# Inverting the 64x64 triangular blocks of a chunked recurrence on 32x32 corners, one PSUM bank a product, with even and odd steps side by side

## The reference

```
proj = h @ w_in                      # h: normed, scaled input
# recurrence, 8 heads of 64, one state of 64x64 a head (rwkv7):
for t in range(1024):
    sa = state @ a_t
    state = state * w_t + sa b_t^T + v_t k_t^T
    y_t = state @ r_t
# and beside it attention over a band of 9 chunks of 64 tokens, 8 heads
x = x + gate * (concat(y_r * silu(g_r), y_a * silu(g_a)) @ w_out)
```

## Time and profile before

| | |
|---|---|
| median of 3 runs | 2421.11 us (2420.31 to 2425.67) |
| profiled execution, own time | 2418.48 us |
| its span, first to last instruction | 2416.6 us |
| PE busy | 2277.8 us, 94% |
| DVE busy | 1456.7 us, 60% |
| ACT busy | 937.6 us, 39% |
| mean granted clock of PE | 0.972 of 2.4 GHz |

### The profile page before, as it was taken

One profiled execution on the slowest core, in us unless ns is written; L12 is line 12 of the kernel. 1 busy time (PEld: TensorE's weight loads), 2 busy tenths in 40 slices (PEclk: granted clock), 3 DMA queues, 4 the chain that ended last, 5 costly groups with the idle time before them and its releaser, 6 DMA issues. The chain is left out here.

```text
span 2416.6 us, 43216 instructions
## 1 busy us (share of the span) xinstructions
PE 2277.8 (94%) x18830; PEld 1848.8 (77%) x18830; DVE 1456.7 (60%) x2456; ACT 937.6 (39%) x1532; POOL 78.7 (3%) x61
## 2 busy tenths in 40 slices
PE   7999988999999999999999999999999998789789
PEld 5777767788888888888878888778777776567667
DVE  5575866565434886777753454646455655767743
ACT  4446432444333443333342433354333232335441
POOL 0000000000000000000000000002000001200000
PEclk9999989999999999999999999989999999799989
DMA  5332252544123232222365534333323113111044
GB/s 179 88 94 66 69 170 71 173 123 129 53 62 119 77 96 83 79 79 86 93 196 164 157 90 135 98 113 110 109 80 107 51 37 97 41 44 44 3 129 150
DMA packets 329349, 238.15 MB, mean 99 GB/s; under 512 B 10948, under 2 KB 288580, under 8 KB 329032
## 3 DMA queue, kind: packets, MB, share of 16 engines
q1 hardware_dynamic: 326424, 229.82, 31.7%
q10 hardware_dynamic: 2736, 5.57, 0.6%
HBM read 202.33 MB, written 33.03 MB: 97 GB/s over the span
## 5 line engine op out<-in xcount | busy, mean ns | idle before, releaser
L1525 PE MATMUL PS<-SR 128*128 128x512 f32 (+2 forms) x1696 | 681.6, 402 | 43.2 <-DVE SR L2106 34.8
L1526 PE MATMUL PS<-SR 128*128 128x512 f32 (+2 forms) x1696 | 659.9, 389 | 0.0
L1527 PE MATMUL PS<-SR 128*128 128x512 f32 (+2 forms) x1696 | 659.7, 389 | 0.0
L2106 DVE TENSOR_TENSOR SR<-SB,SR 128x1024 fp32r<-128x1024 f32 (+1 forms) x240 | 289.1, 1206 | 289.8 <-ACT SR L2967 289.5
L1525 PEld LDWEIGHTS PS<-SR 128*128 128x128 f32 (+1 forms) x1696 | 320.4, 189 | 128.3 <-DVE SR L2106 36.9
L1527 PEld LDWEIGHTS PS<-SR 128*128 128x128 f32 (+1 forms) x1696 | 320.2, 189 | 68.7
L1526 PEld LDWEIGHTS PS<-SR 128*128 128x128 f32 (+1 forms) x1696 | 320.9, 189 | 62.2 <-issue 1.7
L2967 ACT ACTIVATE SR<-SB 128x1024 fp32r<-128x1024 f32 (+1 forms) x240 | 247.5, 1033 | 254.9 <-DMA SB<-in_w_down 116.1
L1546 PE MATMUL PS<-SR 128*128 128x512 f32 x624 | 243.4, 390 | 0.3 <-DVE SR L2232 0.3
L1548 PE MATMUL PS<-SR 128*128 128x512 f32 x624 | 242.8, 389 | 0.0
L1547 PE MATMUL PS<-SR 128*128 128x512 f32 x624 | 242.7, 389 | 0.0
(11 more groups left out here) (315 smaller groups left out, 3032.2 us busy)
## 6 DMA issues: line engine op xcount, KB each, us to landing
SB<-in_w_in SPq DMA_DIRECT2D x110, 512.0 KB, 4.0
SB<-in_w_up SPq DMA_DIRECT2D x88, 256.0 KB, 3.3
SB<-in_w_out SPq DMA_DIRECT2D x32, 512.0 KB, 4.2
SB<-in_w_down SPq DMA_DIRECT2D x32, 512.0 KB, 4.1
SB<-in_w_ada SPq DMA_DIRECT2D x12, 1024.0 KB, 5.2
hidden<-SB SPq DMA_DIRECT2D x22, 512.0 KB, 3.4
SB<-hidden SPq DMA_DIRECT2D x43, 256.0 KB, 5.3
asides<-SB SPq DMA_DIRECT2D x36, 256.0 KB, 4.1
```

The lines of the kernel that those rows point to most:

```text
L1525: pe.matmul(out, whi[:, k - k0, :], hi[k], start=(k == 0), stop=False)
L1526: pe.matmul(out, whi[:, k - k0, :], lo[k], start=False, stop=False)
L1527: i = pe.matmul(out, wlo[:, k - k0, :], hi[k], start=False, stop=(k == j.K - 1))
L2106: v.tensor_tensor(m.f32r(a, kn * cn), m.f32(a, kn * cn), m.f32r(a + 1024, kn * cn).bitcast(F32), SUB).then_inc(*on("split.v", p))
```

## The change

- The inverse is built on 32x32 diagonal blocks in four levels (l = 0..3), with T and TT as compact tiles `Tc` and `TTc` (four 32-row diagonal corners, 256 columns each) in a tile `TB` of their own, and X in `Xc`. A last step (`pre_up` and `pre_add` with l = 4) makes the off-diagonal 32x32 corner of each 64x64 block from the two diagonal ones.
- Each product is 32 matmuls of 32x32 (the last `pre_add` 16) into one PSUM bank, and one DVE instruction of 256 columns drains it. `pre_i` and `pre_t0` go; `pre_mm` makes both M and its transpose on the corners, 64 matmuls in place of 16, and DVE masks them in two instructions and adds the identity in one.
- `pre_own` is new on ACT: four copies of 32 rows from `TTc` into the block diagonal of TT. `pre_add` at l = 4 has one small copy on DVE and one on ACT. `pre_zero` is new on POOL: it clears TT first.
- `seq_u` waits for the three writers of TT.
- `pres(0, 2, 4, 6)` and `pres(1, 3, 5, 7)` are two generators. KN is still one tile, so only one cp at a time is between `pre_kn` and `pre_v` (`masking`).
- The planner's costs of these steps are new, and the projections of k1 and v1 wait for `("read", 2)` and `("read", 3)`.

```diff
-        self.m2, M = f32(X0 + 6656, 640), f32(X0 + 7296, 512)
+        self.m2, TB = f32(X0 + 6656, 352), f32(X0 + 7296, 512)
+        self.TB = [TB, self.fixed["cst"][:, CST["mst"][0]:CST["mst"][0] + 512]]
+        self.Xc = [work(27904, 256), work(28416, 256)]
-        "pre_turn": [("pe", 0.67), ("v", 0.84)], ...
+        "pre_up": [("pe", 0.5), ("v", 0.45)], "pre_add": [("pe", 0.5), ("v", 0.45)], "pre_turn": [("pe", 0.5), ("v", 0.45)], ...
 # Order.pre
-        for l in range(5):
-            yield from one(("pre_up", cp, l), "pre.v", "X", cp, l)
-            if l < 4:
-                yield from one(("pre_turn", cp, l), "pre.v", "T", cp, l)
-            yield from one(("pre_add", cp, l), "pre.v", "TT", cp, l)
+        for l in range(4):
+            yield from single(("pre_up", cp, l), ("pre.v", "X", cp, l))
+            yield from single(("pre_turn", cp, l), ("pre.v", "T", cp, l))
+            yield from single(("pre_add", cp, l), ("pre.v", "TT", cp, l))
+        yield [("pre_own", cp)]
+        yield from single(("pre_up", cp, 4), ("pre.v", "X", cp, 4))
+        yield from single(("pre_add", cp, 4), ("pre.v", "TT", cp, 4), ("pre.a", "far", cp))
 # compose
-                  self.seqs(), self.pres(), ...
+                  self.seqs(), self.pres(0, 2, 4, 6), self.pres(1, 3, 5, 7), ...
 # PE: 32 corners a product
+    def corners():
+        return [(par, j, h, d, slice(64 * h + 32 * d, 64 * h + 32 * d + 32)) for j in range(4) for par in range(2) for h in range(2)
+                for d in range(2)]
+    def pre_turn(cp, l, b, free):
+        w.wait_ge(*at("pre.v", "X", cp, l))
+        w.wait_ge(*at("pre.v", "TT", cp, l - 1))
+        out = corner(b, free)
+        for par, j, h, d, ps in corners():
+            x = pe.matmul(out(ps, par, j), m.TTc[cp % 2][ps, par, j], Xc(cp, ps, par, j), start=True, stop=True)
 # DVE: one instruction in place of two
-        for f in range(2):
-            T = side(m.per[cp % 2]["KN"][:, 0:512], f)
-            v.tensor_tensor(T, side4(bank(got[f][0])), T, ADD).then_inc(*on("pre.v", "T", cp, l, f))
+        v.tensor_tensor(m.Tc[cp % 2], corner(b), m.Tc[cp % 2], ADD).then_inc(*on("pre.v", "T", cp, l))
```

More of the change, by code:

```diff
@@ L693, in flow @@
                 late = max(late, self.placed(step, end if chained else ready))
-                if step[0] not in ("pre_x", "pre_add", "pre_i"):
+                if step[0] not in ("pre_x", "pre_own") and (step[0] != "pre_add" or step[2] == 4):
                     end = late
@@ L1306, in one, with single @@
             yield [use2(step, *release)]
-        yield [("g_load", cp)]
+        def single(step, *releases):
+            yield from self.room((P8, 1))
+            b, free = P8.take()
+            P8.give(b, *releases)
+            yield [(*step, b, free)]
+        yield [("g_load", cp), ("pre_zero", cp)]
         for i in range(2):
@@ L1405, in lora_of @@
         if half:
-            yield from self.after("lo1", "clear", ("read", 3))
+            yield from self.after("lo1", "clear", ("read", 2), ("read", 3))
         else:
@@ L1977, in pre_v @@
             *on("pre.pe", "v", cp))
-    def pre_up(cp, l, got):
-        r = m.per[cp % 2]
-        w.wait_ge(*(at("pre.v", "T", cp, l - 1, 1) if l else at("pre.v", "T", cp)))
-        for par, a, jl, f in crossing(got):
-            j, c, ps = 2 * f + jl, par ^ f, half(par ^ a ^ f)
-            x = pe.matmul(bank(got[f][0])[half(par ^ a), 128 * par + 64 * jl:128 * par + 64 * jl + 64], both(r["AR"])(c, 0, j)[ps, :],
-                          head(r["KN"])(c, 0, j)[ps, :], start=True, stop=True)
-        x.then_inc(*on("pre.pe", "up", cp, l))
@@ L2940, in vector_program @@
               band_y=band_y, mun=mun, prep_a=prep_a, prep_b=prep_b, prep_bon=prep_bon, pre_ar=pre_ar,
-              pre_mm=pre_mm, pre_kn=pre_kn, pre_i=pre_i, pre_t0=pre_t0, pre_up=pre_up, pre_turn=pre_turn, pre_add=pre_add, seq_0=seq_0, seq_x=seq_x, seq_z=seq_z,
+              pre_mm=pre_mm, pre_kn=pre_kn, pre_up=pre_up, pre_turn=pre_turn, pre_add=pre_add, seq_0=seq_0, seq_x=seq_x, seq_z=seq_z,
               seq_mean=seq_mean, seq_var=seq_var, seq_norm=seq_norm, band_p=band_p, seq_out=seq_out, fin_part=fin_part)
@@ L3330, in pre_x, with pre_own, pre_add @@
             S.also("pre.a", "x", cp, 1)
+    def pre_own(cp):
+        w.wait_ge(*at("pre.v", "TT", cp, 3))
+        w.wait_ge(*at("pre.g", "zero", cp))
+        TT = m.per[cp % 2]["TT"].rearrange("p (a j t) -> p a j t", a=2, j=4)
+        for h in range(2):
+            for d in range(2):
+                ps = slice(64 * h + 32 * d, 64 * h + 32 * d + 32)
+                i = a.activation(TT[ps, :, :, 32 * d:32 * d + 32], m.TTc[cp % 2][ps], ACT.Copy)
+        i.then_inc(*on("pre.a", "own", cp))
+    def pre_add(cp, l, b, free):
+        if l == 4:
+            w.wait_ge(*at("pre.pe", "add", cp, 4))
+            w.wait_ge(*at("pre.g", "zero", cp))
+            a.activation(h8(m.per[cp % 2]["TT"])[0:32, :, 32:64], h8(bank(b)[:, 0:256])[0:32], ACT.Copy).then_inc(*on("pre.a", "far", cp))
     def pre_v(cp, got):
@@ L3407, in seq_gain, with pre_zero @@
         g.tensor_tensor(y, y, q, ADD).then_inc(*on("seq.g", "y", cp))
-    do = dict(mark=lambda name: S.mark("g", name), load=load, prep_a=prep_a, prep_b=prep_b, seq_gain=seq_gain)
+    def pre_zero(cp):
+        if cp > 1:
+            w.wait_ge(*at("seq.v", "yr", cp - 2))
+            w.wait_ge(*at("seq.pe", "y", cp - 2, 1))
+        else:
+            for e in S.upto("pe", "gemm0"):
+                w.wait_ge(*e)
+        if cp == 4:
+            for e in (("prep.v", "9", 1, 3), ("prep.g", "c", 1, 3), ("prep.pe", 1, 3)):
+                w.wait_ge(*at(*e))
+        g.memset(m.per[cp % 2]["TT"], 0.0).then_inc(*on("pre.g", "zero", cp))
+    do = dict(mark=lambda name: S.mark("g", name), load=load, pre_zero=pre_zero, prep_a=prep_a, prep_b=prep_b, seq_gain=seq_gain)
     for name, *args in o.steps:
```

169 lines of the change are left out of this document (98 added, 71 removed), and 7 rows, old and new, of the table wide.

## The result

The changed kernel takes 2492.90 us (median of 4 runs, 2490.63 to 2495.39), the kernel before 2420.71 us beside it (2419.45 to 2425.67). The ratio is 1.0295, 95% interval 1.0275 to 1.0314: slower by 3%, where 2388 us was forecast. The profiled execution has a span of 2488.8 us against 2416.6, 72.2 us more.

What follows compares the result with a forecast made beforehand. The end was taken to be set by PE's work plus its waits for the chains. The places summed -5 - 10 - 40 + 22 = -33 on 2418.5 us, 2385.5, plus 2.6 to the median: 2388 us, range 2358 to 2422.

Steps and rivals of the forecast that it cites:

- PE's work hardly changes: +0.4 us a cp: Inverse products of each cp: 13.3 us of PE work against 12.9, +3 us in all.
- My bounds, 7 and 17.5 ns a record: Range around the forecast 11 ns for a 32x32 record: -4 us a cp at about 7, +6.4 at 17.5.
- Place 1: Projections with cp 0 to 3, to 2040 us: idle and tails -10, PE's work +2, stalls +3, together -5 us.
- The +3 of stalls: In the projections: the planner assumes 0.5 us for a product taking 0.86, often with only three matmuls between; +3 us.
- Place 2: 2040 us to `pre_x` of cp 4: `prep_a` starts earlier, table wait stays; -10 us, between -6 and -17.
- Place 3: 2080 us to `most`, cp 4 to 7 and most band units: 168 us of work at 89% filling; -40 us.
- third rival: Bands, not the chain, are the bound: place 3 gains 20 us or nothing; 2408 to 2425 or so, chance 0.08.
- Place 4: `most` to the end: 27 us of band units come here, 5 fit in the 9 us idle; +22 us.
- The drains: One DVE instruction of 0.42 us a product instead of two: 5.2 us saved a cp, DVE's total down about 55.
- The dear matmul: Rival: a 32x32 record costs as much as a 64x64 one, 6.4 us a cp; 2434 us, slower, chance 0.13.
- The queue stalls: Rival: steps placed by a cost of 0.5 us where 0.86 is due; 2413 us at worst, 2405 likely, chance 0.19.

Runs made afterwards that it cites:

- stream kernel: Matmul streams alone on PE (32x32, 64x64, and rounds of a product with 3, 6 or 9 wide matmuls), nothing else computed; the long streams took 55 us each.
- halved kernel: The changed kernel with each level product made by 16 matmuls of 64 rows and 64 weight columns, not the true inverse; 2452.32 us, ratio 1.0122.
- 64x64 kernels: The kernel before with separate T and X tiles, products kept 64x64; two chains 2414.18 us, one chain 2411.47, two chains then one 2399.21.
- 64x64 version with two chains: The kernel before with two generators for even and odd cp and T and X tiles per parity, products kept 64x64; 2414.18 us, ratio 0.9969.
- costs of supply: The changed kernel with the planner's PE costs of products raised to what instruction supply allows (1.8 us for 64 records); 2536.13 us, ratio 1.0471.

## Why the prediction was wrong

**The step that failed** is the sentence "PE's work hardly changes: +0.4 us a cp". It prices an instruction by its execution alone. At the full clock the execution price was about right: 11 ns a record and 0.86 us busy a product were forecast, 10.7 ns and 0.75 us measured in the stream kernel where nothing pauses (`pre_mm` 11.8/8 = 1.47 us, forecast 1.57). In the changed kernel itself a product is 100/108 = 0.93 us busy. But a product is now 64 records and 64 weight loads, 128 instructions, and PE gets 256 in 3.45 us: 1.73 us a product, two and a half times its execution. With 64 instructions, as before, it is 0.86 us against 0.7, and the long matmuls around it make that up, as in the rounds of the stream kernel with 3 of them. My bounds, 7 and 17.5 ns a record, were both bounds of execution; a product's real one, 27 ns a record where products stand densely, was outside them. The stream shows this directly, and the halved kernel and the 64x64 kernels remove it.

The signs were in the trace of before: its queue of instructions brought 10 packets in 55 us of the band stage, about 2500 instructions, and the change added 512 records and 512 weight loads to each cp. The Trainium skill (Runtime: NRT & Kernel Launch, Instruction fetch mechanics) has it that instructions come in blocks of 16 KiB, 256 of them, through a DMA queue of the sequencer's own. The packets of this case agree (256 a packet in the stream). The page calls the cost of crossing a block mostly hidden. That holds for the kernel before (1.4 us of issue waits after 1700 us) and not for the changed one (57.9).

**Place 1**, forecast -5: +18. The idle 6.9 us ahead of k1 did go: k1 follows r1 at 1985.71 with no gap, and the last `pre_add` of cp 3 is at 1945.26. PE waits for DVE no more, but 19.2 us for issue, and it is busy 7 us more. The +3 of stalls was the mis-sized term, and its cause was another.

**Place 2**, forecast -10: -12.5, by the mechanism given. `prep_a` begins at 2042.91, 15.8 us ahead of the end of the projections (2058.7), forecast 16. The wait for the tables is 7.93 us, forecast 9 to 10. The timeline rows:

```profile
2042.91 0.48 DVE L2782 TENSOR_SCALAR SB<-SB 128x512 f32<-128x512 f32 x1
...
2067.43 0.80 PE L1872 MATMUL PS<-SB 64*128 64x128 f32 x4 [7.93 <-DMA SB<-in_band]
```

**Place 3**, forecast -40: +22. I took PE to have 168 us of work and to be filled to 89% by two chains. It is busy 191.2 of 260 us, 74%. So the 62 us between forecast and result are 39 us more idle time and 23 us more busy time. Of the idle time 38.7 us is issue. The busy time is a second thing that I left out: the granted clock of the stretch is 0.82, where it was 0.93 before, which by (1 - 0.82)/0.5 of 260 us means some 94 us at 1.2 GHz, in place of 33. The matmuls of the band units that stayed here would be 75.5 us busy at their mean prices before, and are 86.1; this estimate gives the clock 11 of the 23 us, and most of the rest lies in the recurrence's matmuls, the 0.93 us a product among them. With half the instructions in the same order the clock is 0.91. Whether the pauses or the 32x32 size took it down no run tells apart. Even without the supply, two chains fill little here: with 64x64 products the stretch is 21 us shorter than before, and the units that left it for the final projection are worth as much. That is the third rival, the bands as the bound, to which I had given 0.08.

**Place 4**, forecast +22: +44. The matmuls of the units came about as forecast: 33.4 us among the final projection, 7.2 before, +26. But none of them fit in the idle time ahead of it, which stayed at 8.6 us, and not foreseen was that PE waits in it: busy 125.0 of 140 us, 15 idle, where before it was full. The waits are 9.6 us of the units for their own steps on ACT and DVE, and 4.8 us for a weight split on DVE. In the 64x64 version with two chains the same place took 132 us, so the supply is not its cause. Taking the units out of it (2505.93 and 2425.17 us) brought it to 90 us and cost more ahead of it.

**The drains** were right: one DVE instruction a product at 13.6/32 = 0.42 us, DVE's total down 42 us where I had 55:

```profile
L2878 DVE TENSOR_TENSOR SB<-PS,SB 128x256 f32<-128x256 f32 x32 | 13.6, 424 | 51.0 <-PE PS L2023 50.6
```

It bought no time, since DVE stood idle 51 us ahead of this one group, where before it had stood 11.3 ahead of the same step: it waits for PE's products.

**The rivals.** The dear matmul, 2434 us, would have had the right sign by luck, for the wrong reason: a 32x32 record costs less than a 64x64 one, 10.7 against 19.7 ns (32 records in 0.63 us) in rounds of the same kind. The queue stalls by the planner's costs are not the loss, since the costs of supply made it worse, though the order matters: through the supply, and through the units that it puts among the final projection. Two of the rivals' sums are slightly off (the stalls come to 2415 with their terms of 19 and 11 us in place of the 3, the bands to 2428 with no gain), and 13 drains of 0.42 us save 5.0 us a cp, not 5.2; nothing hangs on them.

What the 32x32 products cost depends on the order. The 64x64 versions differ from these in some steps on DVE and ACT and in the planner's costs too:

| | 64x64 | 32x32 | difference |
|---|---|---|---|
| two chains | 2414.2 | 2492.9 (the changed kernel) | +78.7 |
| one chain | 2411.5 | 2453.8 | +42.3 |
| two chains, then one (32x32: 1.5 us a drain in the table) | 2399.2 | 2436.7 | +37.5 |

With two chains the 79 us are +27, +1, +43 and +7 by place. How the 72 us divide can't be told to the microsecond. 57.9 are issue waits, not all on the path; halving the instructions took back 41 with up to 21 of slower execution against it; the two chains in the band stage cost about 15 (2414 against 2399 us with 64x64 products), and against these stands the gain of places 1 and 2, some 23 us as the 64x64 version has it (329.4 + 39.7 against 320.6 + 25.9).

## What to carry to other kernels

Count instructions, not only their durations. Where PE works through many small matmuls, weight loads included, compare their number in a stretch with the rate at which the queue of instructions can bring them (here 256 in 3.45 us), and spread dense groups among long matmuls. An idle time put down to issue in the middle of a group of like instructions, at a steady distance, is the sign of it. And when two changes come together (smaller products, parallel chains), try each alone at each stage: here the mix of old products, separate tiles, two chains early and one chain late gave 0.9908 of the time before.

## What the runs showed of the hardware

- PE's instructions arrive in packets of 16 KB on their own queue, 256 instructions each, at 3.45 or 3.73 us, rarely 4.0, where they are used up faster; that is 13.5 to 14.6 ns an instruction, 13.9 on the mean of the 32x32 stream. A packet itself takes about 1.1 us of this (14 packets are 1.7% of 16 engines' 55 us).
- The store ahead is small: the 32x32 stream ran 175 records and the 64x64 stream 255, with as many weight loads, before the first pause; 350 and 510 instructions, with what may have come in meanwhile.
- The clock treated two streams with nearly the same pauses differently. The windows of the stream kernel, 32x32 and then 64x64:

```profile
20.00:70.00 50.00, 26.34 (x1792) 24.53 (x1792) 0.00 (x0) 0.00 (x0) 0.53 0.02 5
91.00:140.00 49.00, 29.37 (x1792) 27.41 (x1792) 0.00 (x0) 0.00 (x0) 1.00 0.02 5
```

The 32x32 stream was granted 0.53, nearly all of it at the lower level of 1.2 GHz, the 64x64 stream 1.00, at 2.4 GHz. PE was busy 53% and 60% of the two windows, and in both cases 13 to 14 us of wide matmuls stood ahead. The clock made no difference to their time, since both waited for instructions.
